# A transformer layer and two modulated blocks on one core: the last chunk before each norm run by halves of the rows, x's rows fetched later, the band's mask by memsets

## The reference

```python
x = x + sliding_window_attention(rms_norm(x, mixer_norm), ...)      # 256 rows, 2048 columns, f32
x = x + (silu(h @ w_gate) * (h @ w_up)) @ w_down                    # h = rms_norm(x, ffn_norm)
for l in range(2):                                                  # the second block
    shift, scale, gate = split(silu(c) @ ada_w[l] + ada_b[l])       # three vectors of 2048
    h = rmsnorm(x, g_pre[l]) * (1 + scale) + shift
    if l == 0:
        y = mlstm_mixer(h, ...)                  # 8 heads, w_in 2048 x 16400, w_out 4096 x 2048
    else:
        kmod = silu(c) @ kv_ada_w + kv_ada_b
        hkv = rmsnorm(x, kv_g) * (1 + kmod[2048:]) + kmod[:2048]
        k, v = split(hkv @ kv_w)
        y = band_attention_mixer(h, k, v, ...)   # 16 heads, a band over chunks of 64 rows
    x = x + gate * rmsnorm(y, g_post[l])
```

## Time and profile before

| | us |
|---|---|
| median of 3 runs | 2476.63 (2476.08 to 2476.88) |
| the profiled execution's own time | 2477.34 |
| its span, first to last instruction | 2475.6 |
| PE busy | 2437.5 |
| DVE busy | 1734.6 |
| ACT busy | 1159.6 |
| POOL busy | 44.7 |

### The profile page before, as it was taken

The page is one execution under the profiler, slowest core; times in us unless marked ns, Lnnn a source line. Parts: engine busy times, 40 slices in busy tenths (PEclk is TensorE's granted clock), DMA queues, the critical chain, the costliest instruction groups (busy, mean ns, idle before and its releaser), DMA issues.

```text
span 2475.6 us, 30363 instructions
## 1 busy us (share of the span) xinstructions
PE 2437.5 (98%) x11143; PEld 1990.0 (80%) x11143; DVE 1734.6 (70%) x2394; ACT 1159.6 (47%) x1547; POOL 44.7 (2%) x64
## 2 busy tenths in 40 slices
PE   8999999999999999999999999999999999999997
PEld 6777888888888888788888888888888778888886
DVE  6785777777777776677678667677676576666655
ACT  5565544434443444544444434444444454455553
POOL 1110000000000000000000000000000000000000
PEclk9999999999999999999999999999999999999999
DMA  7434788888888887477777787777776457776653
GB/s 267 138 120 149 253 287 289 304 292 294 290 285 300 291 291 244 137 229 238 239 230 235 243 261 243 240 229 233 246 227 223 144 182 243 248 234 219 215 189 120
DMA packets 161827, 578.13 MB, mean 234 GB/s; under 512 B 18288, under 2 KB 20592, under 8 KB 161680
## 3 DMA queue, kind: packets, MB, share of 16 engines
q1 hardware_dynamic: 160432, 572.64, 70.3%
q0 software_dynamic: 1104, 3.28, 0.5%
q10 hardware_dynamic: 144, 0.26, 0.0%
HBM read 574.01 MB, written 2.10 MB: 233 GB/s over the span
## 4 chain that ended last, share of the span: by engine, by line
PE 92%; DVE 3%; ACT 2%; issue 1%; DMA 1%; SPq 0%; POOL 0%; DVEq 0%; ACTq 0%
PE PS L928 29%; PE PS L930 29%; PE PS L929 29%; PE PS L562 2%; DVE WL L1874 1%; ACT WH L1285 1%; DMA X<-in_x 0%; ACT SQ L963 0%; DVE AR L1394 0%; PE PS L662 0%; PE PS L635 0%; DMA ZG<-in_crow 0%; PE PS L833 0%; PE PS L758 0%; PE PS L778 0%
## 5 line engine op out<-in xcount | busy, mean ns | idle before, releaser
L1874 DVE TENSOR_TENSOR WL<-W,WH 128x1024 fp32r<-128x1024 f32 x816 | 993.6, 1223 | 563.9 <-ACT WH L1285 560.7
L1285 ACT ACTIVATE WH<-W 128x1024 fp32r<-128x1024 f32 x816 | 859.5, 1060 | 950.0 <-PE PS L930 941.5
L928 PE MATMUL PS<-WH,XTH 128*128 128x512 f32 x2144 | 858.5, 400 | 12.0 <-DVE WL L1874 4.7
L930 PE MATMUL PS<-WH,XTL 128*128 128x512 f32 x2144 | 838.3, 391 | 0.0
L929 PE MATMUL PS<-WL,XTH 128*128 128x512 f32 x2144 | 837.0, 390 | 0.0
L928 PEld LDWEIGHTS PS<-WH,XTH 128*128 128x128 f32 x2144 | 403.6, 188 | 103.5 <-issue 18.3
L930 PEld LDWEIGHTS PS<-WH,XTL 128*128 128x128 f32 x2144 | 403.5, 188 | 86.1
L929 PEld LDWEIGHTS PS<-WL,XTH 128*128 128x128 f32 x2144 | 404.1, 188 | 83.1 <-issue 3.8
L928 PE MATMUL PS<-WH,YTH 128*128 128x512 f32 x1120 | 442.1, 395 | 7.6 <-DVE YTL L1407 4.4
L930 PE MATMUL PS<-WH,YTL 128*128 128x512 f32 x1120 | 436.9, 390 | 0.0
L929 PE MATMUL PS<-WL,YTH 128*128 128x512 f32 x1120 | 436.6, 390 | 0.0
(11 more groups left out here) (267 smaller groups left out, 1161.8 us busy)
## 6 DMA issues: line engine op xcount, KB each, us to landing
W<-in_vec SPq DMA_DIRECT2D x192, 512.0 KB, 4.5
W<-in_avoz SPq DMA_DIRECT2D x192, 512.0 KB, 4.5
W<-in_wg SPq DMA_DIRECT2D x88, 512.0 KB, 4.6
W<-in_wu SPq DMA_DIRECT2D x88, 512.0 KB, 4.7
W<-in_wd SPq DMA_DIRECT2D x88, 512.0 KB, 4.7
W<-in_gate SPq DMA_DIRECT2D x64, 512.0 KB, 4.5
W<-in_aqk SPq DMA_DIRECT2D x64, 512.0 KB, 4.7
W<-in_aout SPq DMA_DIRECT2D x64, 512.0 KB, 4.4
```

The lines of the kernel that those rows point to most:

```text
L928: e.matmul(p, x, WH[:, g % NH, j], start=first, stop=False)
L930: i = e.matmul(p, y, WH[:, g % NH, j], start=False, stop=last)
L1285: e.activation(WH[:, n % NH], W[:, i % NW], ACT.Copy).then_inc(s_hi, 1)
L1874: e.tensor_tensor(l, src, h.bitcast(F32), ALU.subtract).then_inc(s_lo, 1)
```

## The change

1. **Halves of the rows.** In the last chunk (c = 3) of the last `down`, of `aout1` and of `bout`, the last four units are run first for row tile 0 and then once more, with the same four converted weights, for row tile 1. The work that follows on tile 0 is put between and beside the second pass. The next chunk after norms 2 and 3 begins with its first four units in the same way (`first_rows`).
2. **The norms' bank** now holds 4 blocks of 128 columns of one row tile: 8 banks (i = 4t + c), in the order 0, 1, 4, 5, 2, 6, 3, 7. `shifted` is four instructions of 128 columns, on ACT for banks 0, 2 and 3, on DVE for the rest; `scaled` is all on DVE. The weights' conversions are called by name (`upper` on ACT, `lower` on DVE). `warm` is gone before norm 2 and is 14 before norm 3.
3. **The last gate row** (c = 3) is multiplied on POOL (`gated`), 128x512 for each row tile.
4. **x's rows** go with tiles 10 to 17; `rows`, `pos`, `cols` after i = 4; `rotary` starts after unit 2; `square_in` 0 comes after unit 7, the others and `stats` after units 1, 3, 4 and 5 of the second chunk; k's ticks in `kv` move by 5 (PE, ACT) and 7 (DVE).
5. **The mask**: no matmul and no `mband`; DVE writes NEG into two 64x64 corners of each head's scores after adding the bias.

```diff
+    def rows(name, ks, par, nk, need, t, after={}):
+        for n, k in enumerate(ks):
+            g = at["g"] + n
+            yield ("slot" if t == 0 and n == 0 else "ready", g)
+            end = "unit" if t else "rows" if k == nk - 1 else None
+            for j in range(2):
+                yield half(g, name, k, j, par, k == 0, k == nk - 1, need(2 * k + j, t), (t,), end)
+            yield ("tick",)
+            yield from after.get(n, ())
+        at["g"] += 4 * t
...
+            if c == 3 and split:
+                at["chunk"] += 1
+                for k in range(nk - 4):
+                    yield from unit(name, k, par, k == 0, False, need)
+                at["rows"] += 1
+                yield from rows(name, range(nk - 4, nk), par, nk, need, 0)
+                yield ("out", out, c, par, at["rows"], (0,))
+                yield from split(lambda after={}: rows(name, range(nk - 4, nk), par, nk, need, 1, after),
+                                 lambda: ("out", out, c, par, at["g"], (1,)))
...
+    def bank(n, i):
+        raw = [("raw", i)] if n == 3 else []
+        return ([("turned", n, i)] + (raw if i >= 4 else []) + [("shifted", n, i), ("upper_T", n, i)]
+                + (raw if i < 4 else []) + [("lower_T", n, i)])
+    def norm_2(second_rows, second_out):
+        g = at["g"]
+        yield ("mean_x", 2, 0)
+        yield ("upper", g + 1)
+        yield ("upper", g + 2)
+        yield ("scaled", 2, 0)
+        yield ("scaled", 2, 1)
+        yield ("lower", g + 1)
+        yield from second_rows({2: [("turned", 2, 0), ("turned", 2, 1)]})
+        for i in (0, 1):
+            yield ("shifted", 2, i)
+            yield ("upper_T", 2, i)
+        yield ("lower_T", 2, 0)
+        yield second_out()
+        yield ("lower", g + 2)
+        yield ("upper", g + 3)
+        yield ("lower_T", 2, 1)
+        yield ("mean_x", 2, 1)
+        yield ("lower", g + 3)
+        for i in (4, 5, 2, 6, 3, 7):
+            yield ("scaled", 2, i)
+        yield from first_rows("X", 2, banks(16), 2)
+    def norm_3(second_rows, second_out):
+        yield ("mean_y", 0, 0)
...
+        for c in range(4):
+            yield ("post", 0, 0, c)
+        yield from second_rows()
+        yield second_out()
+        yield ("mean_x", 3, 0)
+        yield ("mean_y", 0, 1)
+        yield ("upper", g + 3)
+        yield ("scaled", 3, 0)
+        yield ("scaled", 3, 1)
+        yield ("warm", 14)
+        yield ("turned", 3, 0)
+        yield ("turned", 3, 1)
+        yield ("lower", g + 1)
+        yield ("shifted", 3, 0)
+        yield ("upper_T", 3, 0)
+        yield ("post", 0, 1, 0)
+        yield ("post", 0, 1, 1)
+        yield ("lower_T", 3, 0)
...
+    def first_rows(name, n, need, turn_at):
+        late = [bank(n, i) for i in range(8)]
...
+        yield from rows(name, range(4), par, 8, need, 0, {turn_at: late[4], 3: late[5]})
+        fill = [[("upper", g + x), ("lower", g + x)] for x in range(4)]
+        yield from rows(name, range(4), par, 8, need, 1, {0: late[2], 1: late[6] + fill[1], 2: late[3] + fill[2],
+                                                          3: late[7] + fill[3]})
+    def last_rows(second_rows, second_out):
+        yield ("mean_y", 1, 0)
+        for c in range(4):
+            yield ("post", 1, 0, c)
+        yield from second_rows()
+        yield second_out()
+        yield ("mean_y", 1, 1)
+        for c in range(4):
+            yield ("post", 1, 1, c)
...
-    after[1].append(("start", "rotary"))
-    after[7] = [("square_in", 3)]
-    for c, k in enumerate((3, 5, 6)):
-        after[k].append(("square_in", c))
+    after[2].append(("start", "rotary"))
+    after[7] = [("square_in", 0)]
...
-                    e.matmul(b[:, 0:384], idb[:], mband[:], start=True, stop=False)
...
+                    for c in (64, 320):
+                        step(e.memset(s[0:64, c:c + 64], NEG))
+                    settle()
...
+            def gated(p, t):
+                y = YA[:, t, 1536:2048]
+                w.wait_ge(s_sq, SQUARES["y%d" % p, t])
+                w.wait_ge(s_row, 4 * p + 4)
+                e.tensor_tensor(y, y, GG[:, 1536:2048], ALU.mult).then_inc(s_gg, 1)
...
-                if NW <= i < NW + 8:
-                    q = i - NW
+                if 10 <= i < 18:
+                    q = i - 10
...
-                if i == 1:
+                if i == 4:
                     e.dma_start(rows, A["rows"].to_broadcast([128, NROW])).then_inc(s_rows, 16)
```

More of the change, by code:

```diff
@@ L200, in score, with half, unit @@
 def score(plan):
-    at = {"g": 0, "chunk": 0}
-    def unit(name, k, par, first, last, ver, ready):
+    at = {"g": 0, "chunk": 0, "rows": 0}
+    def half(g, name, k, j, par, first, last, need, ts, end):
+        return ("half", g, j, name, 2 * k + j, par, first and j == 0, last and j == 1, need, ts, end if j else None)
+    def unit(name, k, par, first, last, need):
         while at["g"] in plan.folds:
@@ L211, in unit @@
         for j in range(2):
-            yield ("half", g, j, name, 2 * k + j, par, first and j == 0, last and j == 1,
-                   ver + (3 * (k // 2) + 2 + k % 2 if name == "Y0" else k + 1) if ready else 0)
+            yield half(g, name, k, j, par, first, last, need(2 * k + j, 1), (0, 1), "unit")
             if j == 1:
@@ new lines, in norm_3 @@
+    def norm_3(second_rows, second_out):
+        g = at["g"]
+        yield ("mean_y", 0, 0)
+        yield ("upper", g + 1)
+        yield ("upper", g + 2)
+        for c in range(4):
[16 more added lines that the diff above has]
+        yield ("lower_T", 3, 0)
+        yield ("lower", g + 2)
+        yield ("shifted", 3, 1)
+        yield ("upper_T", 3, 1)
+        yield ("post", 0, 1, 2)
+        yield ("post", 0, 1, 3)
+        yield ("lower_T", 3, 1)
+        yield ("lower", g + 3)
+        yield ("mean_x", 3, 1)
+        yield ("raw", 0)
+        yield ("raw", 1)
+        for i in (4, 5, 2, 6, 3, 7):
+            yield ("scaled", 3, i)
+        yield from first_rows("Y", 3, banks(YT_KV), 2)
@@ L282, in score @@
         for c in range(4):
-            yield from chunk("X", 16, h == 0 and c == 0)
+            if h == 0 and c == 0:
+                yield from chunk("X", banks(16), k0=4)
+            else:
+                yield from chunk("X")
             ends.append(last())
@@ L301, in score @@
     for j in range(4):
-        yield from chunk("X", 24, j == 0)
+        yield from chunk("X", pairs(24) if j == 0 else done)
         for _ in range(4 if j else 0):
@@ L867, in tensor_program, with out @@
             added = [0]
[L869 to L870 removed]
+            def out(what, c, par, _, ts):
+                for t in ts:
                     if what in ("aout0", "aout1", "bout"):
@@ new lines, in shifted @@
+            def shifted(n, i):
+                if (n, i) not in ON_ACT:
+                    return
+                b = full(("norm", n, i))
+                w.wait_ge(s_sum, 2 if n == 2 else 4)
+                sc, sh = (COLS[VSC0], COLS[VSH0]) if n == 2 else (COLS[VSCK], COLS[VSHK])
+                for x in range(4):
+                    kt = 4 * i + x
+                    o = e.activation(AT[:, i, x], b[:, 128 * x:128 * x + 128], ACT.Identity,
+                                     scale=mods[:, sc, kt:kt + 1], bias=mods[:, sh, kt:kt + 1])
+                o.then_inc(s_ats, 1)
@@ L1257, in scalar_program, with out @@
             added = [0]
-            def out(what, c, par, _):
-                for t in range(2):
+            def out(what, c, par, _, ts):
+                for t in ts:
                     if what in ("aout1", "bout"):
```

358 lines of the change are left out of this document (187 added, 171 removed).

## The result

The changed kernel takes 2471.4 us (median of 17 runs, 2469.3 to 2472.3), the kernel before beside it 2476.5 (17 runs, 2474.2 to 2478.8): ratio 0.998, 95% interval 0.9972 to 0.9987. The forecast was 2455.5, its range 2445 to 2466. The profiled execution has a span of 2468.5 us against 2475.6.

What follows compares the result with a forecast made beforehand. PE, busy 98% of the span, bounds the kernel by its own work plus its losses. Gains 6.7 + 2.7 + 3.5 + 1.8 + 6.4 = 21.1 us take the median from 2476.6 to 2455.5 us, range 2445 to 2466.

Steps and rivals of the forecast that it cites:

- the part on norm 2: Norm 2: a walk of the queues left 7.4 us lost instead of 9.2, a gain of 1.8 us.
- My bounds: Norm 2: gain 7 if all waits but the first go, loss 3 if each wait drops the clock.
- rival 2: Norms 2 and 3 gain nothing, both gains away: 2463.7 us, chance 0.12.
- rival 5: Low clock stays through both norms, a unit costing 5.1 instead of 2.7 us: 2484 us, chance 0.04.
- The start: First units: waits for x's rows go, 7.2 of 13.9 us stay lost, gain 6.7 us, bounds 1 and 11.
- Rival 1: The start is held by something else: gain there 1.5 instead of 6.7 us, 2460.7 us, chance 0.15.
- Norm 3: Norm 3: 18.4 us lost instead of 24.8, a gain of 6.4 us, bounds 2 and 14.
- The mask: Attention band: 16 mask matmuls go at 0.17 us each, gain 2.7 us; DVE's new memsets are covered.
- The end: After the last matmul: one square step 0.8 and four posts 2.7 us saved, gain 3.5 us.
- It costs nothing in all that range: End: POOL's 128x512 multiply, 0.55 to 1.6 us, taken as 1.2, runs beside the first three posts without cost.
- rival 4: POOL and DVE take turns at the end and in norm 3: about 2 us, 2457.5 us, chance 0.08.
- the rule quoted there: End: skill's shared POOL and DVE SBUF interface, about 2.6 cycles an element; multiply 1.1 us, posts end later.

Runs made afterwards that it cites:

- e1: The changed kernel with the two conversions of the gates' weights moved ahead of norm 2's last banks: 2463.1 us.
- e2: The changed kernel with POOL's set-up of nsel and Ut held back until the gates' weights are made: 2468.6 us.
- e6: The changed kernel with e1's and e2's edits, norm 2's fourth-unit weight before the six scaled, gates' products four x tiles per half-unit instead of two: 2455.7 us.
- e4: The changed kernel with x's DMAs issued four weight tiles earlier again, the squarings left in their new places: 2471.9 us.
- e9: The changed kernel with x's DMAs early as in e4 and the four squarings of x also back at their old places: 2479.0 us.
- e7: e3 with the multiply of the last 512 gate columns on DVE before the last post instead of on POOL: 2454.7 us.
- e3: The changed kernel with norm 2 put back whole as in the kernel before, all else changed: 2455.95 us.
- e11: e6 with e7's edit, norm 3's fourth-unit weight before the six scaled, and norm 2's fifth-unit weight of the chunk before bank 2: 2452.8 us.

## Why the prediction was wrong

**The step that failed** is in the part on norm 2: "Banks 2 and 6, then WL to 25.5: unit 4 waits 1.65. After it WL is just ahead, and the gates' products fill." The gates' products did not fill, they were what PE waited for. I walked DVE's queue with banks and weights and left out the two conversions of the task whose start the change had moved behind the halved norm. e1 shows this alone to be 8.3 us by the medians and 9.1 of the 14.4 by the unit starts. It was in the diff: `("start", "gates")` stands after everything that `norm_2` yields. My bounds (a loss of 3 to a gain of 7) did not hold it, since both were made from the same walk. No rival held it either: rival 2 let the norms gain nothing, rival 5 let them lose only by the clock.

**What else was missing in norm 2.**
- *POOL's set-up beside the six scaled*: 2.8 us (e2, 2.9 by its unit starts). The trace of before already had one of 0.91 us beside the same set-up, where the next took 0.47. In DVE's timeline there:

```profile
1009.52 0.91 DVE L1385 TENSOR_SCALAR AR<-X,st 128x512 f32<-128x512 f32 x1
...
1014.49 0.47 DVE L1385 TENSOR_SCALAR AR<-X,st 128x512 f32<-128x512 f32 x1
```

I used the short duration throughout.
- *The gates' chain behind the chunk*: 4.8 us behind unit 344, with the wait at L856 and the low clock behind it; 1.4 of them went with e1 and are in its 9.1. Before, the gates had 8 units before head 0's mixing, now 4. In e1 the stretch 344 to 360 still costs 3.4, in e6, where the products end two units earlier, 0.7. e6 mended several things at once; that the earlier products alone did it was not tried.
- The steps of a bank were longer than my 1.12 and 1.08: a shift takes 1.5 us on ACT, 1.36 on DVE.

**The start** was right in its cause and 3.9 too small. The waits before units 4 and 6 were 1.65 and 1.36 (forecast 2.3 and 2.0), there was none before unit 7, and the clock cost nothing where I took 1.5. Unit 8 started at 33.3, not 34.3. (The forecast's own terms, 2.3, 2.0, 0.4 and 1.5, add up to 6.2 and not to its 6.5, and its 34.3 leaves out the 1.5 for the clock.) That less traffic would help was not needed (e4). Rival 1 is out: with the squarings back, 9.3 us were lost (e9).

**Norm 3** gained 5.6 of 6.4. The waits were nearly where they were put, but not all of their size: 3.46 for the first bank (forecast 2.8), 0.85 and 2.51 (1.5 and 2.95), and 1.84 where 3.9 were forecast over units 4 to 6. **The mask** gained 2.3 of 2.7, 0.15 a head. **The end** gained 3.0 of 3.5, and that it came so near is in part luck. "It costs nothing in all that range" was wrong: rival 4 holds there and in norm 3, and the four posts with the multiply beside them take 1.05 us longer, all of it on the first. It was offset by 0.6 us from the last post to the end of the span, which I had called the same. Rival 4 was priced at 2 us; e7, which avoids it, gains 0.7 at the end and about as much in norm 3, where that is within the spread. The multiply itself took 1.25 to 1.30 us, and 2.29 once, when it began just after a WL on DVE. I had 1.2, and the rule quoted there, an estimate, 1.1.

So without norm 2's term the sum was 19.3 and 21.5 were gained. 2455.5 was missed by 15.9 us: 16.2 for norm 2, less the 2.2 that the rest gained above its terms, plus the 2.0 by which the medians lie less far apart than the two spans. e3, the changed kernel without that part, came to 2455.95.

## What to carry to other kernels

When a stage is cut into finer steps, list every task whose start stood behind or inside it, also those that the edit doesn't touch, and place each of their instructions in the queues: a conversion of 0.4 us at the wrong place stopped PE for 7. In strict queues the position of an instruction that waits was worth 9 us, the traffic that it waited for nothing. And when two traces run the same units, subtract their starts: this says in one table which term of a sum failed.

## What the runs showed of the hardware

- **POOL and DVE hold each other up**, also when DVE reads one SBUF tensor. A `scaled` of 128x512 took 0.48 us alone and up to 1.32 beside POOL's set-up. A post took 0.74 alone and 1.75 to 1.78 when it began while the 128x512 multiply ran, and the posts behind it took 0.74 again (e7: all sixteen 0.74 to 0.75, with no multiply on POOL). POOL's power of 128x1 took 0.57 and, started 0.16 us after a WL, 1.47; its memset of 8x1024 took 1.17 beside the scaled and 0.94 in e2, where it ran later. The Trainium skill, SBUF — State Buffer, "SBUF: two separate sides", has this as an exclusive lock on one pair of ports, taken by DVE instructions with two SBUF inputs or in a 2-port mode. The trace agrees for the posts, where the whole loss is on the one instruction that began second, and, if `scaled` runs in such a mode (512 elements in 0.48 us is faster than the 0.96 GHz clock of the skill's VectorE: DVE Perf Modes, "Specifications", at one element a cycle), for it too; the mode itself is seen in no row.
- **The clock and short waits.** After the wait of 7.04 us the granted clock was 0.50, the lower of the two levels, and six matmuls took 2.42 us. After that of 3.70 the first six ran at the full rate and the clock was 0.50 only from 1.3 us after PE's start on. In e11 waits of 1.26, 2.26 and 1.25 left it at 1.00 through the whole of norm 2, with no filling matmuls at all, while a wait of 2.04 in e6 was followed by six matmuls and six gate products at the lower level. So the length of a wait alone does not decide it. The same wait, of the same code, went both ways, in e3 (first line) and in e7 (second):

```profile
1001.14 0.74 PE L1076 MATMUL PS<-WH,XTH 128*128 128x512 f32 x1 [2.20 <-DVE XTL L1584]
```
```profile
1001.54 0.47 PE L1076 MATMUL PS<-WH,XTH 128*128 128x512 f32 x1 [2.20 <-DVE XTL L1584]
```

  The granted clock behind it was 0.50 in e3 and 1.00 in e7. It made no difference to the time there, since in e7 PE then waited 1.30 us for the gates' weights, which in e3 it did not. What decides is open.
